# Where the third norm's products stand, and which queue moves x, the rotation tables and y

## The reference

```
mod = c @ w_ada + b_ada ; shift, scale, gate = split(mod)
layer 0: h = rms_norm(x) * (1 + scale) + shift
         q, k, v, g_a, u, g_s = split(h @ w_in_even)
         o_a = attention(rope(q), rope(k), v)     # 64-token chunks, window of 128, sinks
         o_s = state_space(u)                     # 32 groups x 64 complex states, then a GLU
         x = x + gate * ([o_a * silu(g_a), o_s * silu(g_s)] @ w_out_even)
layer 1: b, c, hv, g = split(h @ w_in_odd)        # h from a second norm of x
         x = x + gate * ((silu(g) * b * short_conv(c * hv)) @ w_out_odd)
y = rms_norm(x) * final_g                         # the third norm
```

## Time and profile before

| | |
|---|---|
| median of three runs | 2359.02 us (2357.43 to 2361.9) |
| the profiled execution | 2359.34 us, span 2357.5 us |
| granted TensorE clock, mean | 0.938 of 2.4 GHz |
| TensorE, weight loads, VectorE, ScalarE, GpSimd busy | 2184.6, 1701.3, 814.3, 496.7, 452.0 us |
| moved by the transfers | 414.95 MB, 176 GB/s over the span |

### The profile page before, as it was taken

How to read it: one execution, slowest core, us unless ns; L and a number is a source line. 1 busy time by engine, 2 the same in 40 slices (tenths; PEclk the granted TensorE clock), 3 DMA queues, 4 the chain that set the end, 5 groups by cost and what they waited for, 6 DMA issues and landing times.

```text
span 2357.5 us, 27022 instructions
## 1 busy us (share of the span) xinstructions
PE 2184.6 (93%) x11010; PEld 1701.3 (72%) x11026; DVE 814.3 (35%) x1506; ACT 496.7 (21%) x1030; POOL 452.0 (19%) x319
## 2 busy tenths in 40 slices
PE   7777899899989999999979999999898989999997
PEld 2246666688868757888868677888697767788886
DVE  7332452433334443212325623114134352322232
ACT  1132243322311421001113311002111422200010
POOL 0032623455513201011104011011004000100001
PEclk9988999999989999999989999999868979999998
DMA  7866634798776413654476145554623312343331
GB/s 279 239 239 228 232 143 139 242 311 291 246 288 205 161 72 144 233 195 178 178 214 214 63 163 194 196 190 155 207 91 101 124 36 90 122 147 143 143 138 65
DMA packets 86273, 414.95 MB, mean 176 GB/s; under 512 B 12405, under 2 KB 13461, under 8 KB 51893
## 3 DMA queue, kind: packets, MB, share of 16 engines
q1 hardware_dynamic: 71136, 383.65, 46.1%
q10 hardware_dynamic: 15012, 29.56, 4.4%
HBM read 323.51 MB, written 86.33 MB: 174 GB/s over the span
## 4 chain that ended last, share of the span: by engine, by line
PE 84%; DVE 7%; DMA 3%; POOL 2%; ACT 1%; issue 1%; SPq 1%; ACTq 1%; DVEq 0%; POOLq 0%
PE bank L645 20%; PE bank L647 20%; PE bank L646 20%; PE bank L906 5%; PE bank L666 2%; PE bank L665 2%; PE bank L594 2%; PE bank L864 2%; PE bank L865 1%; PE bank L782 1%; PE bank L740 1%; PE bank L845 1%; PE bank L770 1%; DMA p_rope<-in_rope 1%; DVE p_g L1507 1%
## 5 line engine op out<-in xcount | busy, mean ns | idle before, releaser
L645 PE MATMUL bank<-p_hh,pair 128*128 128x512 f32 x1952 | 790.8, 405 | 68.2 <-ACT p_ut L1074 34.4
L647 PE MATMUL bank<-p_hh,pair 128*128 128x512 f32 x1952 | 776.3, 398 | 0.0
L646 PE MATMUL bank<-p_hl,pair 128*128 128x512 f32 x1952 | 776.0, 398 | 0.0
L645 PEld LDWEIGHTS bank<-p_hh,pair 128*128 128x128 f32 x1952 | 375.4, 192 | 168.8 <-issue 48.9
L647 PEld LDWEIGHTS bank<-p_hh,pair 128*128 128x128 f32 x1952 | 374.6, 192 | 84.7
L646 PEld LDWEIGHTS bank<-p_hl,pair 128*128 128x128 f32 x1952 | 375.7, 192 | 81.3 <-issue 1.4
L445 POOL TENSOR_TENSOR pair<-ring,pair 128x1024 fp32r<-128x1024 f32 x66 | 164.6, 2498 | 211.9 <-ACT pair L436 211.9
L1231 POOL TENSOR_TENSOR pp_mem<-pp_mem 128x512 f32<-128x512 f32 x48 | 62.0, 1293 | 630.8 <-ACT pp_mem L990 630.8
L1320 POOL TENSOR_TENSOR p_g<-p_t,pp_mem 128x512 f32<-128x512 f32 x32 | 41.3, 1290 | 572.5 <-DVE p_t L1772 572.5
L1648 DVE SCALAR_TENSOR_TENSOR p_x<-bank,mod,p_x 128x512 f32<-128x512 f32 x64 | 47.4, 750 | 262.8 <-PE bank L647 262.8
L1746 DVE TENSOR_TENSOR pp_mem<-p_sw,bank 128x512 f32<-128x512 f32 x32 | 22.0, 689 | 305.8 <-PE bank L647 305.6
(11 more groups left out here) (303 smaller groups left out, 2469.1 us busy)
## 6 DMA issues: line engine op xcount, KB each, us to landing
pair<-parts_scratch SPq DMA_DIRECT2D x198, 1024.0 KB, 4.8
parts_scratch<-pair SPq DMA_DIRECT2D x66, 1024.0 KB, 7.5
ring<-in_dense SPq DMA_DIRECT2D x66, 512.0 KB, 5.3
pair<-ssm_scratch SPq DMA_DIRECT2D x24, 1024.0 KB, 6.3
ring<-in_ada SPq DMA_DIRECT2D x24, 512.0 KB, 5.0
p_H<-in_ada SPq DMA_DIRECT2D x24, 512.0 KB, 4.8
p_x<-in_x ACTq DMA_DIRECT2D x4, 2048.0 KB, 16.5
pair<-glu_scratch SPq DMA_DIRECT2D x8, 1024.0 KB, 4.9
```

Source lines behind the costliest of these rows:

```text
L645: pe.matmul(o, ah, bh, start=first, stop=False)
L646: pe.matmul(o, ah, bl, start=False, stop=False)
L647: return pe.matmul(o, al, bh, start=False, stop=last)
```

## The change

The sums of the third norm stand after `u0`, the row after `u1`. The tokens of u go into the memory that attention uses later (`pp_mem`) instead of `prompt.g`; ScalarE waits for the fill of `nb2` instead of the stored y before it issues them, because the third norm's squares and diagonal lie there too. SyncE issues x, the tables and y: in block 1 tables and x behind the raw load of `u1`; in later blocks y of the block before and then x behind the pair of `q1`; the tables of the next block behind the pair of `out0_0`. The last block's y and the sample's y stand before the ten small outputs on SyncE. VectorE waits for the stored y before the first gate writes `prompt.g`.

```diff
--- before.py
+++ after.py
@@ -294,7 +294,6 @@
             S.u0 = 0 if S.prompt else 64
             S.u = u_rows[S.u0:S.u0 + nc_, :, :]
             S.ug = S.u.rearrange("n j m -> n (j m)").rearrange("n (g m) -> n g m", g=GROUPS)
-            S.uj = prompt.g[S.u0:S.u0 + nc_, :, :]
             S.uT = sb(n + "_uT", [P, GROUPS, nc_])
             S.yT = S.uT[:, :, :].rearrange("p (a b) n -> p a (b n)", a=4)
             S.kT = sb(n + "_kT", [P, WINDOW + S.N])
@@ -322,6 +321,9 @@
         S.p = p_mem.rearrange("p (h w) -> p h w", h=NH)
         S.pT = pT_mem.rearrange("p (k h n) -> p k h n", k=2, h=NH)
         S.im = [p_mem[:, 0:NQ * S.NC], p_mem[:, NQ * S.NC:2 * NQ * S.NC]]
+        for S in (prompt, sample):
+            S.uj = pp_mem[S.u0:S.u0 + S.NC, 0:L * 512].rearrange("p (j m) -> p j m", j=L)
+        S = prompt
         S.yc = p_mem[:, 0:2 * TB].rearrange("p (a n) -> p a n", a=2)
         S.pb = pT_mem[:, 0:2 * (TB + 2)].rearrange("p (a n) -> p a n", a=2)
         S.sq = pT_mem[:, 0:2 * TB].rearrange("p (a n) -> p a n", a=2)
@@ -551,16 +553,49 @@
                     src = scratch[1:3, :, at:at + SLOT].rearrange("a p m -> p a m")
                 sp.dma_start(pair[:, s, :, :].bitcast(F32), src).then_inc(pair_in[s], 16)
 
+            def load_x(blk):
+
+                sp.dma_start(prompt.x[:, :, :], xs[0][:, :, blk * TB - TB:blk * TB])\
+                    .then_inc(prompt.sem["x_loaded"], 16)
+
+            def load_rope(blk):
+
+                sp.dma_start(prompt.rope[:, :, :], rope[0][:, :, blk * TB - TB:blk * TB])\
+                    .then_inc(prompt.sem["rope_loaded"], 16)
+
+            def store_y(S, b):
+
+                S.wait(sp, b, "y_ready", 8)
+                dst = y_out[0][:, :, b * TB - TB:b * TB] if S.prompt else y_out[1]
+                sp.dma_start(dst, S.g[:, :, :]).then_inc(S.sem["y_stored"], 16)
+
+            def next_rope(blk, held):
+
+                if held == "out0_0" and blk < NBLK:
+                    prompt.wait(sp, blk, "roped", 5)
+                    load_rope(blk + 1)
+
             for i, held in enumerate(PAIRS + [None] * 3):
                 if isinstance(held, tuple):
                     load_pair(1, held)
                 elif held:
                     load_raw(SPLIT.index(held))
+                if held == "u1":
+                    sp.wait_ge(ada_turned, NROW)
+                    load_rope(1)
+                    load_x(1)
+                next_rope(1, held)
                 if i >= 3 and not isinstance(PAIRS[i - 3], tuple):
                     store_parts(SPLIT.index(PAIRS[i - 3]))
             for blk in range(2, NBLK + 1):
                 for held in PAIRS:
                     load_pair(blk, held)
+                    if held == "q1":
+                        store_y(prompt, blk - 1)
+                        load_x(blk)
+                    next_rope(blk, held)
+            for S, b in ((prompt, NBLK), (sample, 1)):
+                store_y(S, b)
 
             for S, b in ((prompt, NBLK), (sample, 1)):
                 i = S.index
@@ -803,9 +838,9 @@
                                 mm.then_inc(S.fills(b, f"u{t}"), 1)
                         if kp < 3:
                             mm.then_inc(S.sem["u_used"], 1)
+                    if blk > 1 and kp == 0:
+                        norm_sums(prompt, blk - 1, 2)
                     if blk > 1 and kp == 1:
-                        norm_sums(prompt, blk - 1, 2)
-                    if blk > 1 and kp == 3:
                         norm_rows(prompt, blk - 1, 2)
 
                 project(blk, ["k"], streams)
@@ -1061,10 +1096,6 @@
 
             def run_block(blk, streams, last=False):
                 hi = lambda name: split_hi(act, blk, name, streams)
-                act.dma_start(prompt.x[:, :, :], xs[0][:, :, blk * TB - TB:blk * TB])\
-                    .then_inc(prompt.sem["x_loaded"], 16)
-                act.dma_start(prompt.rope[:, :, :], rope[0][:, :, blk * TB - TB:blk * TB])\
-                    .then_inc(prompt.sem["rope_loaded"], 16)
                 hi("k")
                 hi("v")
                 for S, b in streams(blk):
@@ -1073,7 +1104,8 @@
                         o = S.read(act, b, f"u{t}")
                         act.activation(ut(S, t), o[0:S.TP, :], ACT.Copy).then_inc(S.sem["u_copied"], 1)
 
-                    prompt.wait(act, blk - 1, "y_stored", 16)
+                    if S.prompt and blk > 1:
+                        prompt.wait_full(act, blk - 1, "nb2")
                     for t in range(S.NT):
                         S.wait(act, b, "u_copied", t + 1)
                         act.dma_start(S.uj[t * chunks:(t + 1) * chunks, :, :], ut(S, t))\
@@ -1181,10 +1213,6 @@
                         shift(prompt, blk, 0)
                     for S, b in streams(blk):
                         square(S, b, 2, [i])
-                for S, b in streams(blk):
-                    S.wait(act, b, "y_ready", 8)
-                    dst = y_out[0][:, :, b * TB - TB:b * TB] if S.prompt else y_out[1]
-                    act.dma_start(dst, S.g[:, :, :]).then_inc(S.sem["y_stored"], 16)
 
 
             act.wait_ge(dve_built, C_MATRIX)
@@ -1592,6 +1620,8 @@
 
             def gate(S, b, use, n):
                 join(S, b, use)
+                if S.prompt and n == 0:
+                    S.wait(dve, b - 1, "y_stored", 16)
                 o = S.read(dve, b, use)
                 S.wait(dve, b, "tanh_gate", n + 1)
                 dve.scalar_tensor_tensor(out=S.g[:, n, :], in0=S.t1[:, n % 2, :], scalar=1.0, in1=o[:, 0:S.N],
```

## The result

| | before | after |
|---|---|---|
| median of the runs taken side by side | 2358.22 us (2340.51 to 2361.9, four runs) | 2299.42 us (2297.45 to 2302.61, four runs) |
| ratio, 95% interval | | 0.9752 (0.9712 to 0.9792) |
| the profiled execution, its span | 2359.34, 2357.5 us | 2302.61, 2300.7 us |

The change makes the kernel faster by 58.8 us. The forecast was 2315 us (range 2300 to 2330): the direction holds, the gain is 15 us larger than the one worked out, and the time lies just under the range. One of the four runs before, 2340.51 us, lies 17 us under the other three; the experiments come back to it.

A forecast was written before the change was run, and what follows sets the result against it. TensorE, busy 93% of the span, was taken to bound the kernel, leaving gaps and half clock to remove. 2359.3 - 40.4 (seams) - 7 (block 1) + 3 (tail) = 2314.9, forecast 2315 us, range 2300 to 2330.

The forecast's parts named there:

- What bounds: Whole kernel: TensorE busy 93% of the span, so only its gaps and half-clock stretches can come out.
- The seams, 40.4 us: Three seams between blocks: 34.4 us of waits for ScalarE's u copies and 6.0 us of slow clock in k go.
- rival (a): Block 4: the half clock over v goes too, 8.5 us less and a few more; about 2305 us, chance 0.14.
- The tokens: Regrouping of u's tokens at the seams ends before q1 does, margin 3.0 us; costed at nothing.
- SyncE's queue: Later blocks: weights behind y and x, 6.3 million bytes in 20 to 30 us, stay hidden; costed at nothing.
- Block 1, 7 us: Earlier x and tables let q0 start 4.3 us sooner, half clock gives 2.2; gap before xr0 stays; bounds 0 to 12.
- The tail, +3: Kernel's end: ten small outputs now behind y and the sample's y cost 3 us, bounds +0.5 to +4.
- my two cases: Tail: cheapest, ten issues of 0.43 us, +0.5; dearest, third issue taken 5.2 us late, +4.
- (b): Seams and block 1: TensorE waits 3 us in each for the u tokens; 2327 us, chance 0.10.
- (c): Blocks 2 and 3: v falls to half clock as in block 4, twice 10 us; 2335 us, chance 0.07.
- (d): xr0 at each seam: SyncE's queue starves TensorE, 15 us more a seam; 2362 us or more, chance 0.04.
- (e): Seams keep their gap because ScalarE's copies or the bank wait on something else; 2355 us, chance 0.03.

The follow-up runs named there:

- e2: The changed kernel with the third norm's products put back at their old places (sums after u1, row after u3): 2300.17 us, ratio 0.9776.
- e1: The kernel before with the early norm alone (sums after u0, row after u1), queues, token memory and tables as before: 2323.18 us, ratio 0.9878.
- e13: The changed kernel started later, by five loads of x that nothing uses: 2344.02 us, twelve runs.
- e16: The changed kernel with the seam into block 2 alone as it was: 2311.02 us, six runs.
- e7: The changed kernel with x and the tables of block 1 issued by ScalarE at the block's start as before: 2305.77 us, against 2299.51 unaltered.
- e6: The changed kernel with the ten small outputs issued ahead of the last y and the sample's y: 2293.3 us, ratio 0.9714.
- e11: The kernel before with the seam into block 4 alone new, the tokens of u in the new place: 2344.45 us, ten runs.
- e5: The changed kernel with the seam into block 4 alone as it was (late norm, ScalarE issues y, x and the tables): 2311.74 us, six runs.
- e4: The kernel before with the sample's small k product of block 4 behind the prompt's v instead of ahead: 2350.16 us, ratio 0.9992.

## Why the prediction was wrong, point by point

**What bounds.** Right: gaps and half clock were what came out, and the gaps named went.

**The seams, 40.4 us.** The 34.4 us of gap and the 6.0 of slow clock in `k` went as written: `k` takes 5.6 to 5.7 us at 1.00 in all three blocks. By the milestones seams 2 and 3 gave 13.9 and 14.5 us, together 28.4, where my terms for them are 23 + 4.0 = 27.0. That the early norm was needed for it was wrong: I reasoned from one chain, norm, y, issue, copy, and gave the edits one sum; e2 shows that the queue's part alone carries all of it, e1 that the norm's alone leaves 15.0 us of gap.

**The failed step** is the sentence on rival (a): "TensorE was busy through all 20.8 us, and the clock had been up before it fell; what precedes it at once, `k` and the sample's small matmuls, is unchanged", from which I took the half clock of block 4 as part of the kernel, at a chance of 0.14 to go. That TensorE was busy was true, and the conclusion false. It went, and with it 8.2 us in `v` (20.8 to 12.6), 4.6 in the next products (22.1 to 17.5) and 1.2 in the transposes, where I had priced the rival at 10: seam 4 gave 28.1 us, and my terms for it were 11.5 + 1.95 = 13.4. What the runs show in place of that step is that the half clock over `v` hangs on the seams of other blocks: with seams 2 and 4 old 12 of 12 executions are in the upper region, with all seams new none of 15, and one of 12 in e13. By what path stays open. Against the lower level of before, 2343.2 us, the changed kernel is 43.7 us faster, and my sum said 44.4; that `v` is not slowed in that level is taken from its times and no profile shows it, and the nearness is luck in part, since block 1 came out under its term and the stretch near 850 had none. Against the upper level, in which all three runs that I had seen lay (2357.43 to 2361.9), it is 61. Three runs that agree within 4.5 us had made me take the level for the kernel's.

The stretch near 850 (half clock in the gated unit of block 2, 7 us) was of the same kind: it went with the gap of seam 2, as e16 shows, 3.2 us, and no step of mine had it.

**The tokens.** Right, with more margin than written: regrouping ends 21.5 us after the first issue (1165.51 to 1186.96), where I had reckoned with 23.9, and 5.5 us ahead of the first transpose, where I had 3.0. One reading of mine was too strong: with nothing ahead of them on their queue the tokens still made VectorE wait until 19.2 us behind the first issue (1184.68), against 21.6 behind x and the tables, so the 21.6 us say little about the order within that queue.

**SyncE's queue.** Right: no wait of TensorE for weights at a seam. x landed 25.5 us after its issue in the median, and the pairs behind it in time: the stretch from `k` of block 3 to the end of the transposes is busy through all its 30.4 us, with the transfers at a share of 1.05 and 312 GB/s, within the 212 to 314 GB/s that I had used.

**Block 1, 7 us.** The rows gave 6.5; the rest of the 7 had no row. The first two steps hold: `q0` starts when `v` ends (4.2 us) and `q0` and `q1` run at 1.00 (2.2 us). The third does not: I let the gap before `xr0` keep its 5.20 us, and it grew to 7.3, since the raw weights of `q2` and `q3` are now what is late. ScalarE's timeline after:

```profile
212.06 1.06 ACT L438 ACTIVATE pair<-ring 128x1024 fp32r<-128x1024 f32 x1 [17.72 <-DMA ring<-in_dense]
```

Net 4.3 by the profiles, 4 to 6 by e7. The bounds of 0 and 12 held.

**The tail, +3.** Right: +3.0 by the profiles, and 3.0 taken back by e6. The form was between my two cases: four issues of 1.25 us, not one long one.

**The other rivals.** (b) and (c) didn't come: no wait for the tokens, and `v` of blocks 2 and 3 stayed up. (d) and (e) neither. The forecast's own lower bound was loose: its terms give 2359.3 - 40.4 - 12 + 0.5 = 2307.4, and not 2304.

**On the clock.** The rows first: the drop over `v` begins with TensorE busy in every row around it, 3.3 us behind the first of the sample's small matmuls, and e11 has it with no gap ahead, e5 has an 11.5 us gap ahead and no drop. The Trainium skill, "TensorE: Matmul & The Clock Gate", Part 1, says that the default state is throttled and that activity releases it. For the gaps themselves the trace agrees: `k` was slow behind each (0.67, 0.80, 0.75) and is at 1.00 without. For `v` it agrees only as far as e4 goes, whose profile keeps the clock with the small matmuls taken from ahead of it. Read as busy time it does not fit the drop, since TensorE was busy through it; there the measurement decides.

## What to carry to other kernels

Take a large transfer off the issuing program of an engine whose next instruction frees an accumulation bank: a third issue behind 4 MB held ScalarE for 3.87 us at one time and 10.86 at another, and moving the issues gave the whole gain, while making y ready sooner left 15.0 of 34.4 us of gap. Before a stretch at half clock is taken as fixed, ask how many executions show it: repeat the kernel before until its levels are seen, and give a stretch that is at half clock without a gap a fair chance to change whenever gaps elsewhere in the kernel do. Of the three looked at here two went (over `v` and near 850) and one stayed (over the transposes of block 4). Small outputs that are ready belong ahead of the last large store.

## What was not expected of the hardware

- Two levels of one unchanged kernel on one core, 17.6 us apart by their medians, with 66 of 93 executions in the upper; a clock mean of 0.937 against 0.945 tells them apart.
- The half clock over `v`, counted by the executions' times, follows seams of another block: 12 of 12 with seams 2 and 4 old, 0 of 12 with seam 4 alone, 0 of 6 with seam 2 alone, 6 of 6 with seam 3 alone.
- An issue into a queue with 4 MB ahead of it took 11.14, 10.86 and 6.65 us at the three seams where y was issued early (e1) and 3.86 to 3.87 us at all three where it was issued late (before), 1.4 us behind y in all and of the same sizes.
- Behind a 2 MB store the issue of a small one took 1.25 us four times and then 0.43 again.
